# A ninth two-megabyte unit in the ring of expert weights, loop turns of three pairs, and reordered steps of the mixer

## What is computed

```python
h = h + token_mixer(rmsnorm(h, norm_mix), ...)      # w_in, conv, SSD states, attention, w_out
h = h + moe_ffn(rmsnorm(h, norm_ffn), router_w, router_b, w1, b1, w2, b2)
y = rmsnorm(h, norm_final)
# one expert block of moe_ffn:
hcat = xb @ w1[e] + b1[e]                            # 1024 -> 2048
g = minimum(hcat[:, ::2], 7) * sigmoid(1.702 * ...) * (clip(hcat[:, 1::2], -7, 7) + 1)
return g @ w2[e] + b2[e]                             # 1024 -> 1024
```

## Time and profile before

| | us |
|---|---|
| median of 3 runs | 1258.38 (1255.13 to 1261.73) |
| the profiled execution | 1260.86 |
| its span, first to last instruction | 1258.6 |
| PE busy | 1219.2 (97%) |
| DVE busy | 359.5 (29%) |
| ACT busy | 241.2 (19%) |
| POOL busy | 49.2 (4%) |
| DMA | 463.68 MB, 368 GB/s over the span |

### The profile page before, as it was taken

How to read it: one execution, slowest core, us unless ns; L and a number is a source line. 1 busy time by engine, 2 the same in 40 slices (tenths; PEclk the granted TensorE clock), 3 DMA queues, 4 the chain that set the end, 5 groups by cost and what they waited for, 6 DMA issues and landing times.

```text
span 1258.6 us, 14658 instructions
## 1 busy us (share of the span) xinstructions
PE 1219.2 (97%) x5758; PEld 521.2 (41%) x5758; DVE 359.5 (29%) x748; ACT 241.2 (19%) x492; POOL 49.2 (4%) x46
## 2 busy tenths in 40 slices
PE   8999999999999999999999999999999999999997
PEld 6777666544433333333333333333333333333332
DVE  2357434775231221213032121213030221212122
ACT  2014344533211111020111112020111011111103
POOL 0000032512000000000000000000000000000000
PEclk8999999999999999999999999999999999999999
DMA  9576657069799999999999999999999999999995
GB/s 291 171 265 238 210 184 285 22 206 346 301 426 414 428 427 429 428 428 429 429 429 428 428 429 428 429 428 429 429 427 430 427 429 428 428 429 427 430 426 242
DMA packets 64366, 463.68 MB, mean 368 GB/s; under 512 B 7704, under 2 KB 25268, under 8 KB 38380
## 3 DMA queue, kind: packets, MB, share of 16 engines
q1 hardware_dynamic: 62206, 459.16, 88.9%
q10 hardware_dynamic: 1582, 2.22, 0.5%
q0 software_dynamic: 544, 1.84, 0.4%
HBM read 455.95 MB, written 7.24 MB: 368 GB/s over the span
## 4 chain that ended last, share of the span: by engine, by line
PE 76%; DMA 20%; ACT 2%; issue 1%; DVE 1%; SPq 0%; ACTq 0%; DVEq 0%
PE ps L2336 27%; DMA ring<-in_w 19%; PE ps L2360 12%; PE ps L1822 10%; PE ps L2274 5%; PE ps L2126 4%; PE ps L2266 2%; PE ps L2258 2%; PE ps L2260 1%; PE ps L2324 1%; PE ps L1865 1%; PE ps L2344 1%; PE ps L1841 1%; PE ps L2049 1%; PE ps L2166 1%
## 5 line engine op out<-in xcount | busy, mean ns | idle before, releaser
L2336 PE MATMUL ps<-ring,own 128*64 128x512 f32 x1536 | 340.1, 593 | 10.7 <-DMA ring<-in_w 10.7
L2336 PEld LDWEIGHTS ps<-ring,own 128*64 128x64 f32 x1536 | 111.7, 137 | 224.4 <-issue 194.5
L2360 PE MATMUL ps<-ring,own 128*64 128x512 f32 x768 | 171.3, 594 | 4.8 <-ACT own L1093 4.6
L1696 DVE TENSOR_SCALAR own<-ps 128x512 f32<-128x512 f32 x32 | 22.2, 692 | 532.3 <-PE ps L2336 532.3
L1822 PE MATMUL ps<-own,ring 128*128 128x288 f32 x512 | 132.1, 412 | 1.1 <-DVE own L1199 1.1
L2336 PE MATMUL ps<-own 128*64 128x512 f32 x512 | 115.9, 592 | 2.2 <-DMA own<-in_w 2.2
L1822 PEld LDWEIGHTS ps<-own,ring 128*128 128x128 f32 x512 | 96.0, 192 | 30.3 <-issue 4.5
L2360 PEld LDWEIGHTS ps<-ring,own 128*64 128x64 f32 x768 | 56.0, 137 | 111.4 <-issue 109.9
L2274 PE MATMUL ps<-own 128*128 128x512 f32 x180 | 88.5, 617 | 0.0
L1099 ACT ACTIVATE own<-ps 64x512 f32<-64x512 f32 x60 | 35.6, 593 | 206.5 <-PE ps L2360 205.8
L1687 DVE TENSOR_TENSOR own<-ps,own 128x512 f32<-128x512 f32 x34 | 21.9, 686 | 172.4 <-PE ps L2282 172.4
(11 more groups left out here) (371 smaller groups left out, 983.1 us busy)
## 6 DMA issues: line engine op xcount, KB each, us to landing
ring<-in_w SPq DMA_DIRECT2D x143, 2048.0 KB, 30.0
own<-in_w SPq DMA_DIRECT2D x48, 2048.0 KB, 28.6
ring<-in_w_in SPq DMA_DIRECT2D x16, 1024.0 KB, 7.7
ring<-in_cache_win_k SPq DMA_DIRECT2D x8, 1024.0 KB, 5.6
ring<-in_cache_win_v SPq DMA_DIRECT2D x8, 1024.0 KB, 5.0
ring<-in_w_out SPq DMA_DIRECT2D x6, 1024.0 KB, 10.6
ring<-in_state_ssm SPq DMA_DIRECT2D x8, 512.0 KB, 7.6
out_ssm_sample<-ring SPq DMA_DIRECT2D x8, 512.0 KB, 9.7
```

The costliest lines, as they stand in the source:

```text
L1696: nc.vector.tensor_scalar(xg_o, hid[:, 0], LIMIT, None, ALU.min).then_inc(sem("glu_ready"), 1)
L2336: last = nc.tensor.matmul(ps[C * half:C * half + C, 1 + m, :], xT[:, k, C * u:C * u + C], rows[:, D * half + 512 * m:D * half + 512 * m + ...
L2360: last = nc.tensor.matmul(ps[C * half:C * half + C, 4, :], gT[:, (k % 4) * P + C * (k // 4):(k % 4) * P + C * (k // 4) + C], rows[:, 512 * ...
```

## The change

`UNITS` becomes 9. The ninth unit (number 8) lies at the end of `own`, which grows by 3972 words; GpSimd's DMA scratch is cut from 16 KB to 1 KB in each partition to make room. It overlaps nothing of the mixer. Its first load is issued right behind the `w_out` items, before the wait for `M_ready`, and load n + 9 takes the place of load n. Because 9 units and 12 units a pair meet again after 36, a loop turn is three pairs (`TURN = 3`, now counted in pairs): five turns on PE and SP, then the last pair alone, written out. If another pass were needed, three would be run at once; their loads stand unrolled on SP inside an `If` that these inputs jump over.

In the mixer: the rest of the constants is loaded behind the first `w_in` item; PE transposes six of the eight token steps, then the scales and vectors, then the other two; `conv_out` 1 comes behind projection 26; `new_states` has four rounds over banks 4 to 7 in place of eight over banks 4 and 5; and `last_state` comes ahead of them, since banks 6 and 7 must be read before the first round, with its copy on ACT ahead of the biases.

```diff
+PASS_STEP = 3
+MORE_MAX = -(-(MAX_PASS - 1) // PASS_STEP)
...
-UNITS = 8
+UNITS = 9
...
-TURN = 4
+TURN = PASS_STEP
+TURN_UNITS = TURN * PER_PAIR
+FIRST_TURNS = (PAIRS - 1) // TURN
+MORE_TURNS = PASS_STEP * PAIRS // TURN
...
-    put("thresholds", np.tile(C * np.arange(1, MAX_PASS), (P, 1)))
+    put("thresholds", np.tile(C * np.arange(1, MAX_PASS, PASS_STEP), (P, 1)))
...
     steps.extend([("silu", 10), ("silu", 11), ("conv_out", 0)])
     steps.extend(("pv", t) for t in range(3))
-    steps.append(("conv_out", 1))
     proj(26)
-    steps.extend([("ptrans", 4), ("ptrans", 5), ("conv_out", 2), ("p_score", 0)])
+    steps.extend([("conv_out", 1), ("ptrans", 4), ("ptrans", 5), ("conv_out", 2), ("p_score", 0)])
...
-ROUNDS = [(g, half, pair) for half in range(2) for g in range(G) for pair in range(2)]
+ROUNDS = [(g, half) for half in range(2) for g in range(G)]
...
-        WORDS = 28500
+        WORDS = 32472
...
+        spare.append(take(2 * SLOT))
...
-        UNIT_SLOTS = (0, 2, None, 4, None, 6, 8, 10)
+        UNIT_SLOTS = (0, 2, None, 4, None, 6, 8, 10, None)
+        SPARE_OF = {2: 0, 4: 1, 8: 2}
...
             sp.dma_start(h[0:NS, 2, :], a["x_sample"].rearrange("b t d -> (b t) d")).then_inc(sem("x_in"), 16)
-            sp.dma_start(consts[:, 2 * P:], a["consts"][:, 2 * P:]).then_inc(sem("const_in"), 16)
...
+                if n == 0:
+                    sp.dma_start(consts[:, 2 * P:], a["consts"][:, 2 * P:]).then_inc(sem("const_in"), 16)
...
+            def unit_load(expert, n):
+
+                of, which, j = pair_unit(n % PER_PAIR)
+                src = (w1 if which == "w1" else w2)[bass.ds(expert + of, 1), j]
+                sp.dma_start(unit(n % UNITS), src.rearrange("e p c -> p (e c)")).then_inc(unit_full(n % UNITS), 16)
+
+            unit_load(0, UNITS - 1)
             sp.wait_ge(sem("M_ready"), len(BATCHES))
             sp.dma_start(d3(slot(w_out_slot(LAST_W_OUT)), D), w_out[:, 2 * LAST_W_OUT:2 * LAST_W_OUT + 2, :]).then_inc(sem(f"slot_full{w_out_slot(LAST_W_OUT)}"), 16)
...
-                sp.wait_ge(sem("state_new"), 16 * half + 16)
+                sp.wait_ge(sem("state_new"), 8 * half + 8)
...
+            def wait_used(n, turns):
+
+                sp.wait_ge(sem("expert_slot_used"), turns * (2 * TURN_UNITS) + (RING + 2 * (n - UNITS) + 2))
...
-            for n in [3, 0, 4, 2, 1] + list(range(5, PER_EXPERT * TURN)):
+            for n in [3, 0, 4, 2, 1, 5, 6, 7] + list(range(UNITS, TURN_UNITS)):
...
-                turn_loads(q * TURN, q * (2 * PER_EXPERT * TURN))
+                elif 4 < n < UNITS:
+                    sp.wait_ge(sem("expert_slot_used"), UNIT_SLOTS[n] + 2)
+                elif n >= UNITS:
+                    wait_used(n, 0)
+                unit_load(2 * (n // PER_PAIR), n)
+            with sp.Fori(1, FIRST_TURNS) as q:
+                for n in range(TURN_UNITS):
+                    wait_used(n, q)
+                    unit_load(q * (2 * TURN) + 2 * (n // PER_PAIR), n)

...
             with sp.If(more > 0):
                 with sp.Fori(0, more) as p:
...
+                    for turn in range(MORE_TURNS):
+                        for n in range(TURN_UNITS):
+                            wait_used(n, p * MORE_TURNS + (FIRST_TURNS + turn))
+                            unit_load(2 * ((TURN * (FIRST_TURNS + turn) + n // PER_PAIR) % PAIRS), n)
+
+            for n in range(PER_PAIR):
+                wait_used(n, more * MORE_TURNS + FIRST_TURNS)
+                if n < PER_PAIR - 1:
+                    unit_load(NE - 2, n)
...
-            pool.wait_ge(sem("state_new"), 17)
+            pool.wait_ge(sem("state_new"), 9)
...
+            act.wait_ge(sem("turned_ps"), 1)
+            nc.scalar.activation(d3(fin_nat, 512), ps[:, 6:8, :], ACT.Copy).then_inc(sem("read_act"), 1)
+            act.wait_ge(sem("read_act"), 1)
+            act.dma_start(o["ssm_prompt"].rearrange("(j h) p n -> (h p) j n", j=8), d3(fin_nat, N)).then_inc(sem("fin_out"), 16)
             act.wait_ge(sem("b1_rows_in"), 48)
             act.wait_ge(sem("st_ps"), 2)
             act.wait_ge(sem("Bm_ready"), 2)
             nc.scalar.activation(b1p[0:96], b1s[0:96], ACT.Copy).then_inc(b1_parts, 1)
             mixT_evac(1, 1)
-            act.wait_ge(sem("turned_ps"), 1)
-            nc.scalar.activation(d3(fin_nat, 512), ps[:, 6:8, :], ACT.Copy).then_inc(sem("read_act"), 1)
-            act.wait_ge(sem("read_act"), 1)
-            act.dma_start(o["ssm_prompt"].rearrange("(j h) p n -> (h p) j n", j=8), d3(fin_nat, N)).then_inc(sem("fin_out"), 16)
...
-                g, half, pair = ROUNDS[turn]
+                g, half = ROUNDS[turn]
...
-                    old = state[:, b, g, 2 * pair:2 * pair + 2]
-                    nc.vector.scalar_tensor_tensor(old, old, edx[:, 8 * g + b:8 * g + b + 1], ps[:, 4:6, N * (b % 4):N * (b % 4) + N],
+                    old = state[:, b, g]
+                    nc.vector.scalar_tensor_tensor(old, old, edx[:, 8 * g + b:8 * g + b + 1], ps[:, 4:8, N * (b % 4):N * (b % 4) + N],
                                                    ALU.mult, ALU.add).then_inc(sem("state_new"), 1)
...
             add_diagonal(1)
             gated(1, 3)
+            last_state()
             mixT_evac(2, 0)
-            new_states(0)
             mix_scales([(2, 4)], 3)
             scale_tile(1)
+            new_states(0)
             new_states(1)
-            last_state()
-            new_states(2)
             add_mixed(0, 0)
             mixT_evac(1, 0)
+            new_states(2)
+            mixT_evac(1, 2)
             new_states(3)
-            new_states(4)
-            new_states(5)
-            mixT_evac(1, 2)
-            new_states(6)
-            new_states(7)
...
-            for k in range(KT):
+            for k in range(6):
...
             nc.tensor.transpose(ps[:, 1, 0:28], rows_small[0:28, 0:P], ident[0:28, 0:28])
             nc.tensor.matmul(ps[:, 1, 32:112], const("ones")[0:1, :], rows_small[0:1, P:P + 80], start=True, stop=True).then_inc(sem("vecs_to_lanes"), 1)
+            for k in range(6, KT):
+                first_tokens(k)
...
-                g, half, pair = ROUNDS[turn]
+                g, half = ROUNDS[turn]
...
                     pe.wait_ge(sem("yd_out"), 3)
-                for u in range(2):
-                    j = 2 * pair + u
-                    last = nc.tensor.matmul(ps[:, 4 + u, :], Xs[NS * j:NS * j + NS, g, :],
+                    pe.wait_ge(sem("read_act"), 1)
+                for j in range(4):
+                    last = nc.tensor.matmul(ps[:, 4 + j, :], Xs[NS * j:NS * j + NS, g, :],
                                             Bm[NS * j:NS * j + NS, g, 4 * half:4 * half + 4, :].rearrange("p b n -> p (b n)"), start=True, stop=True)
...
-            mixed(0, 0, natural, {2: lambda: diagonal(8), 4: sample_rows, 5: lambda: new_states(0), 8: lambda: new_states(1), 11: lambda: new_states(2)})
+            mixed(0, 0, natural, {2: lambda: diagonal(8), 4: sample_rows, 6: last_state, 8: lambda: new_states(0), 11: lambda: new_states(1)})
...
-            mixed(0, 1, natural, {0: before_1, 1: lambda: new_states(3), 2: lambda: mix_turn(1, 1), 3: lambda: new_states(4), 4: last_state,
-                                  5: lambda: new_states(5), 6: lambda: mix_turn(1, 2), 7: lambda: new_states(6), 9: lambda: new_states(7)})
+            mixed(0, 1, natural, {0: before_1, 2: lambda: mix_turn(1, 1), 4: lambda: new_states(2), 6: lambda: mix_turn(1, 2), 8: lambda: new_states(3)})
...
             h_turn(0, 0)
-            pe.wait_ge(sem("read_act"), 1)
+            pe.wait_ge(sem("state_new"), 4 * len(ROUNDS))
...
             wait_mixT(pe, 1, 2)
-            pe.wait_ge(sem("state_new"), 4 * len(ROUNDS))
...
-                turns = t * (16 * (PER_EXPERT * TURN // UNITS))
+                turns = t * (16 * (TURN_UNITS // UNITS))
...
-                        if ending and n == PER_EXPERT * TURN - 1 and k % W2_ROWS == 2:
+                        if ending and n == PER_PAIR - 1 and k % W2_ROWS == 2:
...
-                pairs = [t * (TURN // 2) + r for r in range(TURN // 2)]
+                pairs = [t * TURN + r for r in range(1 if ending else TURN)]
                 for r, pt in enumerate(pairs):
                     first = PER_PAIR * r
-                    closing = ending and r == TURN // 2 - 1
...
-            turns_before_last = more * (NE // TURN) + (NE // TURN - 1)
+            turns_before_last = more * MORE_TURNS + FIRST_TURNS
             with pe.Fori(0, turns_before_last) as t:
                 expert_turn(t, False)
...
-    nc = bacc.Bacc("TRN2", target_bir_lowering=False, num_devices=1)
+    nc = bacc.Bacc("TRN2", target_bir_lowering=False, num_devices=1, dynamic_dma_scratch_size=1024)
```

More of the change, by code:

```diff
@@ L55 @@
 W2_UNITS = 2
-TURN = 4
+TURN = PASS_STEP
+TURN_UNITS = TURN * PER_PAIR
+FIRST_TURNS = (PAIRS - 1) // TURN
+MORE_TURNS = PASS_STEP * PAIRS // TURN
+assert TURN_UNITS % UNITS == 0 and (PAIRS - 1) % TURN == 0
```

(47 more changed lines are left out.)

19 lines of the change are left out of this document (8 added, 11 removed).

## The result

| us | before | after |
|---|---|---|
| median | 1258.38 (4 runs, 1255.13 to 1261.73) | 1246.78 (4 runs, 1246.03 to 1248.17) |
| the profiled execution | 1260.86 | 1248.17 |
| its span | 1258.6 | 1246.4 |
| PE busy | 1219.2 | 1211.5 |

The ratio is 0.9916 (95% interval 0.9891 to 0.994): the changed kernel is **faster by 0.84%, some 10.5 us** (7.6 to 13.7 by the interval); the medians differ by 11.6. Forecast were 1248.8 and 0.76%.

The account below looks back on a forecast made before the run. The prediction took the saturated 428 GB/s weight stream as the bound, ending 16.5 us after PE alone would. Its terms, -4.9 - 1.8 - 0.7 - 2.2 = -9.6 us, gave 1248.8 us, range 1243 to 1259 with C left out.

Parts of the forecast that it names:

- The bound: Experts: the saturated 428 GB/s weight stream sets the end; only more bytes loaded before it or an earlier begin helps.
- PE's wait for data: Experts: the kernel ends 16.5 us later than PE alone would; 11.6 us remain after the ninth unit's 4.9.
- The ninth unit: Weight ring: an extra unit loaded behind `w_out` puts all later loads one unit ahead; -4.9 us, bounds 0 and 4.9.
- empty slice: Slice 8 of the profile, 220 to 252 us, at 22 GB/s: the ninth unit's load takes 4.9 us of it.
- Turns of three pairs: Expert loop: a turn's end costs PE 0.14 us, and SP's jump over unrolled loads is hidden; 0.
- C: Rival, expert loop: the three-pair body no longer stays with PE, fetch stalls at turn ends; 1271.7 us, chance 0.10.
- `conv_out` 1: Mixer: placed behind projection 26, PE's 1.92 us wait for ACT's copy vanishes; -1.8 us, bounds 0 and -1.9.
- Token steps: Start: scales before the last two transpose steps fill PE's 1.07 us idle time; -0.7 us, bounds 0 and -1.1.
- Constants: Start: loading them behind the first `w_in` costs nothing, since they are read 10 us later at the earliest; 0.
- Rounds and `last_state`: Mixer: four rounds save 4.2 us, waiting before `last_state` costs 1.7; -2.2 us taken, bounds +1.7 and -4.2.
- POOL and ACT behind the later sum: Mixer: POOL's bias subtraction waits some 2 us longer; ACT's 6.58 us idle before the samples' norm covers it.
- The sum: Whole kernel: the parts add to -9.6 us, giving 1248.8 us against the median of 1258.38, 0.76% less.

Follow-up runs that it names:

- `mixer_only`: The changed kernel with eight units and the old turns and scratch, keeping the new mixer order; 1249.69 us, ratio 0.995 to before.
- `unit_only`: The changed kernel with the mixer undone, keeping the ring of nine and turns of three pairs; 1251.05 us, ratio 0.9965 to before.
- `late_ninth`: The changed kernel with the ninth unit's first load issued behind unit 7 instead of behind `w_out`; 1243.73 us, ratio 0.9913 to before.
- `after_again`: The changed kernel itself run again, on the same chip as `late_ninth`; 1245.8 us, ratio 0.9916 to before.
- `rounds_undone`: The changed kernel with eight rounds over two banks and `last_state` behind them again; 1248.33 us, ratio 0.9938 to before.
- `consts_undone`: The changed kernel with the constants loaded ahead of the first `w_in` item again; 1245.54 us, ratio 0.9911 to before.
- `warm8`: The changed kernel with eight warm-up products on PE before the tokens in place of six; 1245.44 us, ratio 0.9909 to before.
- the body with 48 more: The changed kernel with 48 semaphore increments added to PE's loop body per turn; 1242.96 us in one run.
- the body with 144 more: The changed kernel with 144 semaphore increments added to PE's loop body per turn; 1246.35 us in one run.
- the two longer bodies: The changed kernel with 288 or 768 semaphore increments added to PE's loop body per turn; 1252.19 us (one run) and 1380.29 us.
- `half_ninth`: The changed kernel with load n = 9 in two halves, the first sent once PE has read half of unit 0; 1247.09 us, ratio 0.9907 to before.

## Why the prediction was right

**The bound.** Both halves of the argument hold: shortening PE's way to the experts and adding bytes ahead each move the end in full, the first in `mixer_only`, where the last column stays, the second in `unit_only`, where only the last column shrinks. PE's wait for data did shrink as forecast: 1180.96 - (326.90 + 15 x 56.15) = 11.8 us by the reckoning of the forecast, which had 11.6. The nearness is partly luck: the prediction's pace was 0.09 us too slow. Every second pair of before takes 0.14 to 0.2 us more than the first, and with turns of three this is gone (56.06 each; the cause is open); by that pace 13.2 us are left. So PE gained 1.4 us more on its way through the pairs, and they went into its wait: at the end at most the 0.3 of the next paragraph show.

**The ninth unit, -4.9.** Measured -5.2: the kernels with eight units have 924.66 and 925.24 from the first expert product to the end; the eight of these runs with nine and a plain or slightly longer body (after, `unit_only`, `late_ninth`, `after_again`, `rounds_undone`, `consts_undone`, `warm8`, and the body with 48 more, 919.57) have 919.06 to 920.33, mean 919.76; the body with 144 more, whose first pair is 0.9 us longer, has 920.3. That it fell into the empty slice was true and not needed.

**Turns of three pairs, 0.** The first pair of a turn follows within 0.01 us. The stall that C names cost 2.7 and 5.9 us a turn in the two longer bodies, around the 4.2 us from which I had it decide; the 6.9 us taken from a 128 KB transfer were above both. The trace of before could not show how close the edge was. The Trainium skill's two figures (Runtime: NRT & Kernel Launch, "Instruction fetch mechanics") fare as the prediction put it: two blocks of 16 KB do not fit the missing fetches of three pairs either. Room for 2048 instructions does fit: my count of 1470 matmul and weight-load instructions leaves 578 for waits and the rest, and the edge was met between 144 and 288 added.

**`conv_out` 1, -1.8.** Measured -1.9: the stretch up to `w_out` goes from 227.7 in `unit_only` (228.1 in before) down to 225.8 (226.3 in `mixer_only`), and the wait of 1.92 is gone.

**Token steps, -0.7.** Some -0.5 to -1.3, by the clock of the execution. No run undoes this step alone, but traces at the same clock can be compared. From the first transposes to the convolution's it is 16.0 us in `unit_only`, which has the old order, and 14.8 and 14.9 in `after_again` and `half_ninth`, whose mean clock from 7 to 24 us is 0.90 as well; before and after, both at 0.53 in the window above, have 18.2 and 17.7. Where the clock did not fall it is 13.2 with the new order, and no execution of the old with such a clock was profiled. The stretches at the lower level don't lie at quite the same times in these pairs, so the size is rough. **Constants, 0**: as measured.

**Rounds and `last_state`, -2.2.** Measured -3.0; the one term clearly mis-sized. Row groups: four cost what two did (1.14 against 1.13), as taken from L1906. The Trainium skill's table (TensorE: Matmul & The Clock Gate, "Why this matters for your kernels") has four such tiles 3.07 times as fast as one by one, from which the prediction estimated a third more for a round; the traces don't show that third. The wait of PE came as described and cost 1.54 for the 1.7 forecast. I had taken 0.3 off for the last round's DVE part; nothing of that shows, and without it the two terms give -4.2 + 1.54 = -2.7. The other 0.3 is in the products with `w_out` themselves, a term that the prediction did not have: between the first of them and `h_turn` the same 48 records stand in 11 groups where before had 15, and they take 22.0 us in place of 22.4, counted from start to start in the two timelines.

**POOL and ACT behind the later sum.** Covered: after, the norm of the samples on ACT (L819, timeline) still finds 1.52 us of idle time.

```profile
292.50 1.06 ACT L819 ACTIVATE own<-own 32x1024 f32<-32x1024 f32 x1 [1.52 <-DVE own L1547]
```

But it was 6.58 us before, so most of the cover is used, and the next such step may find none. The 2 us that the prediction gave to the later sum were too few: POOL's subtraction (L789 at 277.42 before, L795 at 275.42 after) stands 12.1 us ahead of `h_turn` before and 7.6 after, so it moved by 4.5.

**The sum.** Terms at equal clock: -5.2 - 1.9 - 3.0 and -0.5 to -1.3 make -10.6 to -11.4; the ratio gives -10.5 and the medians -11.6; forecast -9.6. The ratio's own interval of 6 us can't tell these apart; the stretches can. No term had the wrong sign, and none came back as a wait elsewhere, because the end was set by one quantity, bytes ahead of the stream, that all of them move.

## What to carry to other kernels

Where a kernel ends with a saturated stream, count the bytes loaded before it begins and the moment it begins; a saving on the engine's way there is then worth its full size, and another buffer is worth its transfer time, wherever an idle stretch of the queue can take it. Before lengthening a loop body, look for fetches in a window deep in the loop: none there says only that this size fits, and a stall of 2 to 6 us per turn may be some 200 instructions away. Where runs of one program differ by several us, find the stretch in which they part, and compare kernels only behind it.

## What the runs showed that I had not expected

- The same program gets a mean granted clock of 0.53, 0.84 or 1.00 between 10 and 21 us, worth up to 5 us of 1246, half of what the whole change brings; two more warm-up products don't alter it.
- PE keeps a body of three pairs, and 144 instructions more, with not one fetch in 440 us; 288 more bring nine fetches a turn and 2.7 us, in steps and not gradually. The price is one stop at the turn's end, and behind such a stop the granted clock can fall as well.
- A transfer begun 1.72 us earlier, while the queue stood empty, brought 0.4 MB ahead, and 30 us after the first expert product all of it was given back.
- GpSimd's 544 packets (1.84 MB, the page's line of queue q0) run from a scratch of 1 KB with no loss that any stretch of the table shows.
